# Solves and states of a tile moved into the first half of the next turn, behind the next tile's first Gram

## The chip, the core and the metric

The kernel runs on one core of one Trainium2 chip. The metric is device time of one execution in microseconds (us): the median of three runs, beside one profiled execution whose trace is read here. Engines: PE (TensorE) multiplies, PEld is its weight load, DVE (VectorE) and POOL (GpSimd) do elementwise work, ACT (ScalarE) activations and copies out of PSUM, SP issues the DMAs of this stage.

## What is computed

One inference step of a hybrid decoder layer over 1024 prompt tokens and 64 sample tokens (8 sequences of 8), all fp32, D_MODEL 1024:

```python
proj = rmsnorm(x) @ w_in
conv_out = swish(LayerNorm(causal depthwise conv of width 31 (GLU)))
# rwkv group, 8 heads of 64, per token t:
S_t = S_{t-1} diag(w_t) + (S_{t-1} (-kk_t)) (kk_t*a_t)^T + v_t k_t^T
y_t = S_t r_t                     # then per-head GroupNorm + bonus, output gate
x = x + concat(conv_out, rwkv_out) @ w_out
x = x + HierMoE(RMSNorm(x))       # 32 experts, top-2 in the top-1 group
```

The change lies wholly in the stage that computes the recurrence S_t, y_t. The recurrence is done in chunks of 64 tokens: within a chunk a unit triangular matrix is built from products of the keys (a Gram matrix) and inverted, and then the chunk's corrections u, its outputs y and the new state follow from a few 64x64 products per head.

## The kernel before

Programs of the engines are written out by hand; their order is the order of the calls, and semaphores tie them. After the input projection a loop of **turns** works on tiles of 128 tokens (NT - 1 = 8 tiles of the prompt, and tile 8 with the 64 sample tokens). In turn j (`turn(j)`, one function of that name on each engine) four tiles are in work:

- tile j + 1: `decay`, `iclr`, `key_norms`, `cumulate` on PE, `decay_tanh`, `iclr_tanh`, `norms_wide`, `exps`, `key_scale` on ACT, `decay_add`, `keys`, `scaled_a_b` on DVE, `scaled_r_k` on POOL. The last two make the operands of the next turn's Gram; PE waits for them in `scaled_ready`.
- tile j: `gram_and_values` (first Gram, banks 2 and 3, and value transposes, bank 0), `first_level` and `first_gb` on DVE, the key Gram and `key_tokens`. The 16x16 diagonal blocks of its triangular matrix are inverted on DVE (`small_blocks`, `whole_blocks`), with SP carrying them out to DRAM and back in another layout (`invert_blocks(j)`: 8 stores at L604, 2 loads at L608, then, when `blocks_turned` on ACT is done, 2 stores at L613 and 8 loads at L618).
- tile i = j - 1: with its inverted blocks in place (`inv_in`), two levels of doubling make the inverse of 64x64 (called level 4 and 5; PE products, DVE `level_masks`, ACT `x_copies`). Then a chain in two chunks: PE `first_u`, ACT `u_copy`, PE `first_state`, DVE `new_state`, PE `second_rhs`, ACT `rhs_copy`, PE `second_u`, ACT `u_copy`, PE `second_state`, ACT `y_copy`.
- tiles j - 2 and j - 3: GroupNorm (`gn_centre`, `gn_square`, `gn_variance`, `gn_root`, `gn_inverse`, `y_scaled`), `to_channels`, `gn_affine`, the bonus and the `gate`.

On PE all solves, state and output products go through L1704 (`product`), Grams are L1730, transposes into tokens L1716, decay and iclr L1568 and L1574, `key_norms` L1582, `cumulate` L1659. On DVE: `level_masks` L2636, `keys` L2473 and L2478, `small_blocks` L2650 and L2652, `new_state` L2674 and L2677, `whole_blocks` L2661 to L2669, `scaled_a_b` L2487 and L2492, `gn_centre` L2684 and L2685, `gn_variance` L2692. On ACT: `exps` L1132 to L1134, `key_scale` L1065, `u_copy` L1232, `blocks_turned` L1077, `gn_root` L1249 (a Sqrt, for which ACT loads another table), `norms_wide` L1072, `tok_copy` L1210. On POOL: `scaled_r_k` L848 to L860, `r_times_k` L885, `y_plus_bonus` L898.

Turn j of PE ends with the chain of tile j - 1, and turn j + 1 begins with `scaled_ready` and the first Gram of tile j + 1; then PE needs the inverted blocks of tile j (`level_in`, `inv_in`). ACT's `blocks_turned(j)` stands near the end of turn j, behind `exps`, `key_scale` and the second `u_copy`. DVE's `whole_blocks(j)` uses the tile MM as scratch and so waits for the last read of MM by PE.

## Time and profile before

| | us |
|---|---|
| median of 3 runs (lowest, highest) | 1180.27 (1179.73, 1181.55) |
| the profiled execution | 1184.61 |
| its span, first to last instruction | 1182.8 |
| PE busy | 1074.6 (91%) |
| DVE, ACT, POOL busy | 665.6, 356.4, 213.6 |
| mean granted TensorE clock, as a share of 2.4 GHz | 0.959 |

The turns lie between 386 and 617 us of the span; before them is the input projection, behind them the output projection and the experts. The page gives the busy share of each engine in 40 slices of 29.6 us, and the clock that PE was granted; the trace gives every instruction with its start, its length and what released it. The fall of the clock to a half is seen as a PEclk of 0.50 over a short window. Between the profiled execution and the median lie 4.3 us.

### The profile page before, as it was taken

The numbers are of one execution on the slowest core, as the hardware profiler recorded it, in microseconds if no ns is written. First come the engines' busy times: TensorE is split into PE (matmuls) and PEld (weight loads), VectorE is DVE, ScalarE is ACT, GpSimd is POOL, SyncE is SP. The second block draws the span as 40 slices with busy tenths as digits, with TensorE's granted clock in tenths as the row PEclk, the third lists the DMA queues.
The fourth block names the chain that finished last, engine by engine and source line by source line (L and its number), as shares of the span: only waits on it lengthen the run. The fifth ranks groups of instructions, "written<-read, shape, count | busy, mean of one in ns | idle before, by whom it ended". The sixth has DMA issues, their size and how long they took to land.

```text
span 1182.8 us, 24194 instructions
## 1 busy us (share of the span) xinstructions
PE 1074.6 (91%) x9392; PEld 636.7 (54%) x9393; DVE 665.6 (56%) x1136; ACT 356.4 (30%) x691; POOL 213.6 (18%) x278
## 2 busy tenths in 40 slices
PE   7999999999997767777689999985999999999986
PEld 5666666666665766766685455554333333333342
DVE  6388999973668666666543321456434343343416
ACT  6000011101335555555432221113132323222324
POOL 4000000000011312222220011001333333242110
PEclk9999999999998888898999999986999999999999
DMA  9211111100000111111124322138898889999839
GB/s 277 65 35 36 36 36 44 33 27 22 1 1 8 23 21 19 18 19 20 20 48 188 106 63 71 45 120 339 326 377 317 323 311 342 414 406 404 329 115 389
DMA packets 97790, 171.44 MB, mean 145 GB/s; under 512 B 44490, under 2 KB 69249, under 8 KB 88419
## 3 DMA queue, kind: packets, MB, share of 16 engines
q1 hardware_dynamic: 90211, 152.31, 36.2%
q0 software_dynamic: 7488, 17.84, 4.3%
q8 instruction: 66, 1.08, 0.4%
q14 instruction: 25, 0.20, 0.1%
HBM read 153.64 MB, written 25.91 MB: 152 GB/s over the span
## 4 chain that ended last, share of the span: by engine, by line
PE 79%; DMA 8%; DVE 4%; SPq 3%; ACT 3%; issue 2%; POOLq 0%; DVEq 0%; ACTq 0%
PE ps L1688 27%; PE ps L2306 13%; PE ps L2156 9%; PE ps L2336 7%; PE ps L1704 7%; SPq L618 2%; DMA arena<-y_rows 2%; PE ps L2293 2%; DMA arena<-in_w_exp_up_dram 2%; DMA x_blocks<-arena 2%; PE ps L2186 1%; DMA arena<-x_blocks 1%; PE ps L1730 1%; DMA arena<-in_w_exp_down_dram 1%; ACT arena L1065 1%
## 5 line engine op out<-in xcount | busy, mean ns | idle before, releaser
L1688 PE MATMUL ps<-arena 128*128 128x384 f32 (+1 forms) x1032 | 316.6, 468 | 0.0
L1688 PEld LDWEIGHTS ps<-arena 128*128 128x128 f32 x1032 | 195.3, 190 | 118.0 <-issue 1.9
L2306 PE MATMUL ps<-arena 128*64 x416 | 188.5, 596 | 3.0 <-DVE arena L3040 1.4
L2309 PE MATMUL ps<-arena 128*64 128x512 f32 x416 | 188.5, 596 | 0.0
L2458 DVE SCALAR_TENSOR_TENSOR arena<-arena,cw 128x1024 f32<-128x1024 f32 x240 | 168.2, 777 | 0.4
L1704 PE MATMUL ps<-arena 64*64 64x64 f32 x2960 | 101.9, 240 | 57.6 <-DMA arena<-x_blocks 35.9
L1704 PEld LDWEIGHTS ps<-arena 64*64 64x64 f32 x2960 | 92.9, 153 | 63.8 <-issue 44.1
L2306 PEld LDWEIGHTS ps<-arena 128*64 128x64 f32 x416 | 54.4, 136 | 111.8 <-issue 111.6
L2156 PE MATMUL ps<-arena 128*128 128x512 f32 x256 | 113.1, 596 | 0.0
L2336 PE MATMUL ps<-arena 128*64 x208 | 96.5, 607 | 2.4 <-ACT arena L1443 2.4
L2339 PE MATMUL ps<-arena 128*64 128x512 f32 x208 | 96.5, 607 | 0.0
L2156 PEld LDWEIGHTS ps<-arena 128*128 128x128 f32 x256 | 47.5, 190 | 57.1 <-issue 57.0
L964 POOL DMA_INDIRECT late<-xn_rows,g_idx x24 | 65.9, 2744 | 20.4 <-POOL g_idx L961 20.4
L870 POOL COPY lastz<-arena 128x1 f32<-128x1 f32 x14 | 11.4, 813 | 318.0 <-ACT arena L1161 318.0
L1155 ACT ACTIVATE arena<-ps 128x768 f32<-128x768 f32 x14 | 11.4, 812 | 178.6 <-PE ps L1688 178.6
L3061 DVE COPY arena<-arena 128x4096 f32 x26 | 59.4, 2283 | 8.5 <-SPq L707 6.7
L3046 DVE TENSOR_TENSOR small<-ps,small 128x256 f32<-128x256 f32 x26 | 11.0, 424 | 89.6 <-ACT small L1427 89.6
L2336 PEld LDWEIGHTS ps<-arena 128*64 128x64 f32 x208 | 26.8, 138 | 53.0 <-issue 53.0
L3070 DVE COPY arena<-ps 128x256 f32<-128x256 f32 x26 | 11.0, 424 | 78.1 <-PE ps L2322 78.1
L1443 ACT ACTIVATE arena<-arena 128x2048 f32 x26 | 49.6, 1908 | 17.5 <-SPq L711 16.3
L2309 PEld LDWEIGHTS ps<-arena 128*64 128x64 f32 x416 | 54.4, 136 | 0.0
L1730 PE MATMUL ps<-arena 64*64 64x128 f32 x544 | 41.6, 313 | 6.9 <-DVE arena L2492 6.9
(370 smaller groups left out, 1490.3 us busy)
## 6 DMA issues: line engine op xcount, KB each, us to landing
arena<-in_w_exp_gate_dram SPq DMA_DIRECT2D x32, 1024.0 KB
arena<-in_w_exp_up_dram SPq DMA_DIRECT2D x32, 1024.0 KB
arena<-in_w_exp_down_dram SPq DMA_DIRECT2D x32, 1024.0 KB, 9.4
arena<-in_w_in_dram SPq DMA_DIRECT2D x22, 512.0 KB, 4.1
arena<-in_x_prompt_dram SPq DMA_DIRECT2D x16, 512.0 KB, 8.2
arena<-y_rows SPq DMA_DIRECT2D x8, 1024.0 KB, 16.3
arena<-in_w_out_dram SPq DMA_DIRECT2D x2, 2048.0 KB
xn_rows<-arena SPq DMA_DIRECT2D x8, 512.0 KB, 2.9
```

Source lines behind the costliest of these rows:

```text
L964: pool.indirect_dma_start(out=xg[b], out_offset=None, in_=xn2_rows, in_offset=bass.IndirectOffsetOnAxis(ap=g_idx[b][:, :], axis=0), bounds ...
L1443: act.activation(wd.rearrange("p c n -> p (c n)"), wring[:, bass.ds(slot, 1), 2 * DC * F:].rearrange("p a n -> p (a n)"), ACT.Copy)\
L1688: ins = pe.matmul(banks(proj_bank(q) + piece)[:, 0:n1 - n0], win[q % 6][:, c, :], xnT[:, c, n0:n1], start=(c == 0), stop=(c == DC - 1))
L1704: ins = pe.matmul(dst[h, hp * 64:hp * 64 + 64], lhs[k, hp, :], rhs[k, hp, :], start=alone or (first and hp == 0), stop=alone or last, skip ...
L1730: ins = pe.matmul(banks(2 + c)[half(p), hp * P:(hp + 1) * P], lhs[h, hp, t], AR[j % 3][h, hp, :, t], start=True, stop=True)
L2156: ins = pe.matmul(banks(2 * (i % 2) + half)[0:r, :], lhs, wout[c // CT][:, c % CT, half * 512:half * 512 + 512], start=(c == 0), stop=(c = ...
L2306: pe.matmul(banks(b)[0:HS, :], xgT[b][:, c, 0:HS], wring_gu[:, bass.ds(slot, 1), 0:2, c, :].rearrange("p a w f -> p (a w) f"), start=(c == ...
L2309: ins = pe.matmul(banks(b)[HS:P, :], xgT[b][:, c, HS:P], wgu[b][:, :, c, :], start=(c == 0), stop=(c == DC - 1))
L2336: pe.matmul(banks(5 + half)[0:HS, :], hT[:, c, 0:HS], wring[:, bass.ds(slot, 1), n0:n0 + 512].rearrange("p a n -> p (a n)"), start=(c == 0 ...
L2339: ins = pe.matmul(banks(5 + half)[HS:P, :], hT[:, c, HS:P], wd[:, c, half * 512:half * 512 + 512], start=(c == 0), stop=(c == 1))
L2458: dve.scalar_tensor_tensor(out=dst, in0=src, scalar=w, in1=dst, op0=ALU.mult, op1=ALU.add).then_inc(conv_tap, 1)
L3061: dve.tensor_copy(wgu[b].rearrange("p w c f -> p (w c f)"), wring[:, bass.ds(slot, 1), 0:2 * DC * F].rearrange("p a n -> p (a n)"))\
```

## The change

- The chain of tile m = j - 2 (u, state, y of both chunks) is issued in a new first half of turn j, not in the second half of turn j - 1. PE's order there: `scaled_ready(j)`, first Gram and values of tile j, `chain_u`, `chain_state`, decay and iclr of tile j + 1, `chain_rhs`, `second_u`, `to_channels(j - 3)`, `bonus(j - 1)`, `second_state`, `gate(j - 3)`, `key_norms(j + 1)`, then level 4 of tile j - 1.
- ACT's `blocks_turned(j - 1)` moves to the first half of turn j, behind `u_copy`, `gn_root`, `norms_wide` and `tok_copy`.
- DVE: `new_state` of tile j - 2 around `first_gb(j)`; `bonus_v`, `keys` and `gated` ahead of the level 5 masks; `gn_centre` behind them; `scaled_a_b(j + 1)` between `small_blocks(j)` and `whole_blocks(j)`.
- POOL: `r_times_k` ahead of `y_scaled`.
- Tiles that now live longer get another buffer: a third value and a third GB1 tile, a fourth e_last; `whole_blocks` gets scratch of its own and no longer waits for PE; the decay product goes to bank 4, the gate to bank 0. The constant headmean, which nothing used, goes, with its three memsets.
- The last turn of the prompt has both: the chain of tile 6 in its first half and, as before, that of tile 7 in its second.

```diff
 # PE
+            def chain_u(m):
+                pe.wait_ge(rhs_done, n + 1)
+                pe.wait_ge(x_done, level_count(m, 5, 1))
+                pe.wait_ge(tok_done, 3 * m + 5)
+                for hp in range(CT):
+                    ins = solve_u(m, 0, hp)
+            def chain_state(m):
+                pe.wait_ge(u_done, n + 1)
+                for hp in range(CT):
+                    rhs_keys(m, 1, hp)
+                    ins = state_u(m, 0, hp)
+            def chain_rhs(m):
+                pe.wait_ge(gb_done, m + 3)
+                pe.wait_ge(s_done, n + 2)
+                for hp in range(CT):
+                    y_keys(m, 0, hp)
+                    ins = rhs_state(m, 1, hp)
+                ins.then_inc(rhs_psum, 1)
+                pe.wait_ge(rhs_psum, n + 2)
+                for hp in range(CT):
+                    y_state(m, 0, hp)
+                    y_keys(m, 1, hp)
+                for hp in range(CT):
+                    ins = y_u(m, 0, hp)
+            def first_half(j):
+                m = j - 2
+                scaled_ready(j)
+                if j < NT - 1:
+                    gram_and_values(j)
+                else:
+                    gram(j, bt, gb_psum)
+                if j >= 2:
+                    chain_u(m)
+                    chain_state(m)
+                if j < NT - 1:
+                    if j == 1:
+                        pe.wait_ge(cvar_done, len(PIECES))
+                    if j >= 4:
+                        pe.wait_ge(aff_done, j - 3)
+                    decay(j + 1, decay_bank(j + 1))
+                    pe.wait_ge(kk_done, 2 * j + 1)
+                    iclr(j + 1)
+                if j >= 2:
+                    chain_rhs(m)
+                    second_u(m)
+                if j < NT - 1:
+                    if j >= 3:
+                        pe.wait_ge(decay_sum, j + 2)
+                        to_channels(j - 3, 4)
+                    bonus(j - 1)
+                if j >= 2:
+                    second_state(m)
+                if 3 <= j < NT - 1:
+                    pe.wait_ge(tok_done, 3 * j + 1)
+                    gate(j - 3, 0)
             def turn(j):
-                scaled_ready(j)
-                gram_and_values(j)
-                pe.wait_ge(kk_done, 2 * j + 1)
-                pe.wait_ge(s_sum, n)
-                decay(j + 1, decay_bank(j + 1))
-                iclr(j + 1)
+                first_half(j)
+                pe.wait_ge(iclr_done, j + 2)
+                key_norms(j + 1)
+                pe.wait_ge(decay_sum, j + 2)
+                pe.wait_ge(rk_used, j)
...
                 pe.wait_ge(tok_done, 3 * j + 1)
+                if j >= 3:
+                    pe.wait_ge(mix_done, j - 2)
                 key_tokens(j)
...
-                pe.wait_ge(iclr_done, j + 2)
-                key_norms(j + 1)
                 level_x(i, 5)
-                first_u(i)
-                if j >= 3:
-                    to_channels(j - 3, 4)
-                else:
-                    bonus(i)
-                first_state(i)
-                if j >= 3:
-                    bonus(i)
-                second_rhs(i)
+                pe.wait_ge(tok_done, 3 * j + 3)
                 cumulate(j + 1)
-                second_u(i)
-                if j >= 3:
-                    gate(j - 3, 4)
-                second_state(i)
 # ACT
+            def first_half(j):
+                m = j - 2
+                if j >= 2:
+                    u_copy(2 * m)
+                if j >= 3:
+                    gn_root(j - 3)
+                if j == 3:
+                    conv_root(2)
+                if j < NT - 1:
+                    norms_wide(j + 1)
+                    tok_copy(j, 0, value_rows(j), 0)
+                if j >= 2:
+                    blocks_turned(j - 1)
+                if j < NT - 1:
+                    iclr_tanh(j + 1)
+                if j >= 2:
+                    rhs_copy(2 * m + 1)
+                if j < NT - 1:
+                    decay_tanh(j + 1)
+                if j >= 2:
+                    y_copy(m, 0, 2)
+                    u_copy(2 * m + 1)
+                    if 3 <= j < NT - 1:
+                        gn_affine(j - 3, 4)
+                    y_copy(m, 1, 3)
 # DVE
             def turn(j):
                 first_level(j, mask_ar)
+                if j >= 2:
+                    new_state(j - 2, 0)
                 first_gb(j, mask_ar)
-                level_masks(j - 1, 4)
+                if j >= 3:
+                    gn_inverse(j - 3)
                 decay_add(j + 1)
                 if j >= 2:
-                    gn_centre(j - 2)
+                    new_state(j - 2, 1)
+                bonus_v(j - 1)
+                level_masks(j - 1, 4)
+                keys(j + 1)
                 if j >= 3:
-                    gn_inverse(j - 3)
+                    gated(j - 3, 0)
                 masked_k(j, mask_ar)
                 level_masks(j - 1, 5)
-                keys(j + 1)
+                if j >= 2:
+                    gn_centre(j - 2)
                 small_blocks(j)
-                new_state(j - 1, 0)
+                scaled_a_b(j + 1)
                 whole_blocks(j)
-                bonus_v(j - 1)
-                scaled_a_b(j + 1)
-                new_state(j - 1, 1)
-                if j >= 3:
-                    gated(j - 3, 4)
                 if j >= 2:
                     gn_variance(j - 2)
```

## Rows read from the trace of the kernel before

**Rows 1.** The page, second part: PE's granted clock in 40 slices, in tenths.
```profile
PEclk9999999999998888898999999986999999999999
```

**Rows 2.** Waits from 410 to 592 us: who for whom, us, times, longest.
```profile
PE ps L1704 <- DMA arena<-x_blocks: 35.7, 7, 6.5
```

**Rows 3.** Windows: stretch, its us, busy (x) of PE, PEld, DVE, ACT, POOL, PEclk.
```profile
418.60:446.00 27.40, 19.30 (x618) 17.87 (x622) 17.98 (x41) 15.68 (x35) 4.42 (x4) 0.87 0.13 20
446.00:591.30 145.30, 106.32 (x3236) 98.33 (x3236) 95.34 (x215) 80.95 (x184) 39.60 (x36) 0.91 0.12 19
591.30:616.60 25.30, 24.66 (x632) 23.32 (x632) 9.46 (x19) 10.45 (x27) 7.42 (x6) 0.89 0.26 51
```

**Rows 4.** Timeline of turn 5: PE's first level-4 product, SP's issues; landing of L608.
```profile
504.47 1.34 PE L1704 MATMUL ps<-arena 64*64 64x64 f32 x35 [4.77 <-DMA arena<-x_blocks]
...
499.07 3.75 SPq L618 DMA_DIRECT2D arena<-x_blocks  x8
...
509.01 1.15 SPq L608 DMA_DIRECT2D arena<-u_blocks  x2
...
528.77 2.27 SPq L618 DMA_DIRECT2D arena<-x_blocks  x5
...
DMA to landing us min/median/max: 2.0/2.7/3.8
```

**Rows 5.** Timeline of DVE in turn 5: start, us, line, tiles, idle before and releaser.
```profile
508.15 0.69 DVE L2685 SCALAR_TENSOR_TENSOR arena<-arena 128x512 f32<-128x512 f32 x1
...
510.95 0.89 DVE L2636 TENSOR_TENSOR arena<-ps,mask_lv 128x256 f32<-128x256 f32 x2 [0.25 <-PE ps L1704]
...
513.83 0.17 DVE L2650 TENSOR_TENSOR arena<-arena 128x12 f32<-128x12 f32 x1
...
516.18 0.17 DVE L2652 TENSOR_TENSOR arena<-arena 128x12 f32<-128x12 f32 x1
...
517.83 1.64 DVE L2663 TENSOR_TENSOR arena<-arena 128x256 f32<-128x256 f32 x1
...
519.96 0.59 DVE L2663 TENSOR_TENSOR arena<-arena 128x256 f32<-128x256 f32 x1
...
521.01 0.41 DVE L2669 TENSOR_REDUCE arena<-arena 64x32 f32<-64x256 f32 x1
...
524.42 0.68 DVE L2492 SCALAR_TENSOR_TENSOR arena<-arena 128x512 f32<-128x512 f32 x1
...
528.60 0.67 DVE L2692 TENSOR_REDUCE arena<-arena 128x8 f32<-128x512 f32 x1
```

**Rows 6.** Timeline of ACT around the end of turn 5.
```profile
522.00 0.60 ACT L1132 ACTIVATE arena<-ps 128x512 f32<-128x512 f32 x1 [0.43 <-PE ps L1659]
...
523.45 1.64 ACT L1065 ACTIVATE arena<-arena,om_ka,prm 128x128 f32<-128x128 f32 x4
524.99 0.38 ACT L1232 ACTIVATE arena<-ps 128x256 f32<-128x256 f32 x1
525.25 0.63 ACT L1077 ACTIVATE arena<-arena 64x256 f32<-64x256 f32 x1
...
527.02 1.28 ACT L1249 ACT_TABLE_LOAD   x1
529.31 0.30 ACT L1249 ACTIVATE arena<-arena,stat 128x8 f32<-128x8 f32 x1 [1.01 <-DVE arena L2692]
...
530.03 0.58 ACT L1210 ACTIVATE arena<-ps 128x512 f32<-128x512 f32 x1
```

**Rows 7.** Timeline of POOL in turn 5.
```profile
517.76 1.27 POOL L898 TENSOR_TENSOR arena<-arena 128x512 f32<-128x512 f32 x1 [6.43 <-ACT arena L1258]
...
525.17 1.27 POOL L853 TENSOR_TENSOR arena<-arena 128x512 f32<-128x512 f32 x1 [0.63 <-ACT arena L1065]
```

**Rows 8.** Windows over first Gram and values, in turns 1 and 2, at either clock.
```profile
386.20:389.80 3.60, 3.60 (x65) 3.27 (x65) 0.97 (x2) 1.81 (x3) 3.15 (x3) 0.50 0.21 21
410.80:412.70 1.90, 1.90 (x74) 1.73 (x68) 1.66 (x2) 0.90 (x2) 1.82 (x3) 1.00 0.26 71
```

## What was expected of the change

> **What bounds the kernel now.** I read the page's slices first. PE is busy nearly everywhere, but in the stage of the turns its granted clock is below full in most slices [rows 1], and only there does the clock fall again and again. Next the waits of that stage: PE waits 35.7 us in 7 pieces for the inverted blocks that SP brings back from DRAM [rows 2]. Then the windows: from one level 4 to the next, turn 2 takes 27.4 us and turns 3 to 7 take 145.3 us, 29.06 each, of which PE is busy 106.32 us, 73%, at a mean clock of 0.91; turn 8 has no such wait left in it, 24.66 of 25.3 us are busy [rows 3]. So in turns 2 to 7 PE's work is not the limit, a loop is, and the reader finds it by following the blocks. In turn 5 (I write T for the start of level 4, 504.47): the loads of the inverse began 5.40 us earlier; the second trip of SP, which brings the raw blocks, starts at T + 4.54 [rows 4]; DVE's level 5 masks end at T + 7.4, after them come the keys, `small_blocks` starts at T + 9.36 and ends at T + 11.9, and `whole_blocks` ends at T + 16.95 [rows 5]. ACT turns the blocks only at T + 20.78 to T + 21.4, because exps, key_scale and a u_copy stand ahead of it [rows 6]; the loads start at T + 24.3 [rows 4], and 5.4 us later the next level 4 can start, T + 29.7. That is the turn. PE's idle time hides in this loop, and so does part of its half clock.
>
> **What the change does to the loop, step by step.** The same sum for a turn 3 to 6 after the change, T again at level 4.
>
> (a) Start of `small_blocks`. The raw blocks: T + 4.54, the second issue some 0.6 later, landing 2.7 after it [rows 4]: T + 7.8. DVE: the level 5 masks; keys, 1.8, and the gate product, 0.6, are moved ahead of them, but into time in which DVE waited for PE, and PE has lost nothing there except that `key_tokens` now waits for `gated`. I lay these at T + 4.2 for the gate product, 5.3 for the tokens, 6.9 for the end of the masks (estimate: 7.4 in rows 5 with the first 3.4 us at half clock, less 1.2 for that, plus 0.7 for the new wait). Then `gn_centre`, 1.3 (two operations like the one in rows 5). T + 8.2, so DVE and not the DMA decides, by 0.4. Bounds 7.8 and 9.4 (as before).
>
> (b) `small_blocks`, 2.4 (513.83 to 516.35) [rows 5]: T + 10.6.
>
> (c) `scaled_a_b`, new at this place, 2 operations of 0.68 overlapping a little [rows 5], 1.3: T + 11.9. It needs the exps, and these need `cumulate`, which PE can now issue right behind level 5, about T + 7.4 to 8.5; exps until T + 10.1. They are ready. PE's next turn starts here, because `scaled_ready` waits for it: PE is idle from T + 8.5 to T + 12.
>
> (d) `whole_blocks`. In turn 5 it takes 3.8 us (517.62 to 521.42) though one of its two equal multiplications took 1.64 and the other 0.59 [rows 5]: the long one began at 517.83 and ended 0.44 behind POOL's operation, which ran from 517.76 to 519.03 [rows 7]. Bare, it is 2.8. Moved, it lies at T + 11.9, and key_scale ends at T + 11.6 (exps at 10.1 and 1.64 [rows 6]); 0.08 behind that start POOL's two products of `scaled_r_k`, 1.27 each [rows 7], then `r_times_k`. So where there was one overlap there are now two or three: 0 to 2.1 us, and I take 2.1, since the start of the POOL operation follows key_scale by a fixed 0.08 and the copy and first multiplication fall just behind it. T + 16.8. The Trainium skill (SBUF — State Buffer, section Practical consequences) says why, and speaks against this place: a DVE instruction with two SBUF inputs contends with a GpSimd instruction that reads SBUF, and the later one is blocked to the end of the first. By that rule the 2.1 is due in full; had the rule no hold here the sum would be 2.1 less. The trace agrees with it, 1.64 against 0.59.
>
> (e) `gn_variance` 0.65 [rows 5], and ACT's `gn_root` with `norms_wide`, `tok_copy` and `blocks_turned` behind it: from 529.27 (end of the variance) to 530.61 [rows 5, 6] and another 0.63, 2.0. T + 19.5.
>
> (f) SP: stores, loads, landing: 2.9 (525.88 to 528.77) and 5.4 [rows 4, 6], 8.3. T + 27.8.
>
> There is a second path into (e), through PE and ACT, and it is the one that I trust least. `blocks_turned` stands behind `u_copy(2m)`, and that behind the first Gram: T + 12, Gram and values 1.9 at full clock or 3.6 at half [rows 8], the solve 0.6 to 1.1, the copy 0.5 with its latencies [rows 6], the table load of 1.28 that follows [rows 6], then the 2.0 of (e): T + 18.3 or T + 20.4; with (f) T + 26.6 or T + 28.7. Will the clock be half there? PE's idle time of 3.5 us is shorter than the 4.77 us that came before a fall [rows 4], and longer than any ahead of the Gram of turn 2, which ran at full clock [rows 8]. I expect a fall in part of it, and a turn of **28.2 us**, between 27.8 and 28.7.
>
> PE's own path has more air: `chain_rhs` starts when DVE is through with the variance, `first_level`, `new_state` and `first_gb`, about T + 19.8; then the rhs copy (behind `iclr_tanh` in ACT's queue, T + 23.2), the second solve, the u copy at T + 25, `new_state` and `bonus_v` until T + 27.1, gate and key_norms until T + 27.6. 0.6 us ahead of the blocks. The idle 4.8 us of PE are thus filled with the chain, but two other waits (3.5 and 1.2 us, with 0.5 before `first_gb`) take their place. The waits that are added for bank 4 and bank 0 (`aff_done`, `decay_sum`) end earlier than this and cost nothing; the memsets taken out stand in the start and cost or give nothing.
>
> **The sum over the turns.** Turn 2: no gate product and one more small root, 27.9 against 27.4. Turns 3 to 6: 28.2. Turn 7: the next tile has 64 tokens, so scaled_a_b and POOL's products are half as long, and norms_wide and tok_copy are not ahead of `blocks_turned`: 25.6. Together 27.9 + 4 * 28.2 + 25.6 = 166.3, against 27.4 + 145.3 = 172.7: -6.4. Turn 1 loses nothing of its chain (tile 0's goes to turn 2), its key norms and bonus come ahead of level 4, +1.8, but `blocks_turned(1)` has no root ahead of it: I get level 4 of turn 2 1.4 us earlier. Turn 8 is PE work, 24.66 of 25.3 us at a mean clock of 0.89 [rows 3]; its level 4 began behind 6.5 us of idle time [rows 2], now about 3: of the loss of 2.8 (0.11 * 25.3) I count half as regained, -1.4. Sum -9.2. What follows (output projection, routing, experts) waits for nothing with a date of its own, its loads hang on this stage's semaphores, so all of it is passed on: 1184.6 - 9.2 = 1175.4 for the execution as profiled, and from the median 1180.3 - 9.2 = **1171**. The first is 4.3 above the second before the change; I keep that distance.
>
> **The rivals.**
> - *The overlaps do not come and the clock holds.* Then (d) costs 2.8 and the PE path decides, T + 26.6: 5 * 26.6 + 24.4 = 157.4, -15.3, with -1.4 and -2.8, -19.5: 1161. For it: in rows 7 POOL's start hangs on ACT, and 0.3 us of shift would let DVE go first. Against: the idle 3.5 us of PE.
> - *The loop stays as long as it was.* Half clock in all of the chain and small_blocks only at T + 8.9: the turn stays near 29, the six sum to 172, and turn 8 gives nothing: with turn 1 some 1178, 1177 to 1180. For it: before the change, too, the loop went through DVE, ACT and SP, none of which gets less work. That the gain is made but not passed on to the end would look the same.
> - *Slower: the first Gram ahead of the solve.* PE could solve tile m at T + 8.5, where all inputs are there, but must wait for `scaled_a_b`, and ACT's table load and `blocks_turned` queue behind the copy of that solve. If small_blocks starts at T + 9.4 as before, PE starts at T + 13.1, and with half clock: 3.6, 1.1, 0.5, 1.3, 2.0 and 8.3 make T + 29.9. Five of these and one of 27.5 make 177, +4.3, and turn 1 gives nothing either: 1185. It decides as soon as the first solve's copy ends after T + 18 or so, against T + 17.2 in my sum.
>
> **How the numbers follow.** The forecast, own range 1167 to 1176, 0.45; the fast case 0.20; the unchanged one 0.17; the slower one 0.15; 0.03 for cases between the first two. A measurement of this kernel can tell about 0.2%, 2.4 us, from no change, so faster begins at 1177.9: of the unchanged case 0.03 lies below that and 0.01 above 1182.7. Faster 0.71, same 0.13, slower 0.16. Leaving out one in ten at either end, the range is 1160 to 1183.
>
> **What would show it.** Right: level 4 starts 28.2 us apart; PE's longest idle time in a turn lies before the first Gram and is about 3.5 us, released by DVE L2492; its wait for x_blocks is near 1 us; the copy and multiplications of `whole_blocks` are stretched beside POOL's products; turn 8 starts at full clock. Wrong: small_blocks later than T + 8.5, for then (a) is mis-sized; blocks turned later than 2.0 us behind `gn_variance`, for then ACT's queue holds them; or turns of 30 us with the wait for x_blocks still 4 us.

## The result, and the profile after

| | before | after |
|---|---|---|
| median of the runs beside each other | 1180.91 (1179.73 to 1182.38, 4 runs) | 1200.62 (1199.03 to 1203.87, 4 runs) |
| the profiled execution, its span | 1184.61, 1182.8 | 1201.09, 1199.3 |
| mean granted clock | 0.959 | 0.952 |
| the end of turn 8 in the span | 616.5 | 633.6 |

The changed kernel is slower: 1.017 times the time before, interval 1.0145 to 1.0195, some 20 us. The spans differ by 16.5 us, and at the end of turn 8 the difference is already 17.1, so all of it arises in the turns, and what follows passes it on but for 0.6 us. The traces are of single executions: that of the kernel before lies 4.3 us over its median and that of the kernel after 0.5, so the medians differ by 19.7 us where the traces differ by 16.5. The page of the kernel after:

```profile
PE 1083.2 (90%) x9392; PEld 643.5 (54%) x9393; DVE 676.3 (56%) x1136; ACT 356.8 (30%) x691; POOL 214.9 (18%) x275
...
PEclk9999999999997988888899999995999999999999
```

The clock row answers rows 1: it still falls in the slices of the turns. DVE's work is busy for 676.3 us where it was 665.6, though it computes the same; the extra time will turn up below. Next PE's waits from 405 to 640 us (for whom, us, times, longest), beside rows 2:

```profile
PE ps L1746 <- DVE arena L2554: 31.4, 7, 6.8
PE ps L1720 <- DMA arena<-x_blocks: 7.3, 6, 2.9
PE ps L1720 <- ACT arena L1232: 7.1, 5, 1.7
PE ps L1720 <- DVE arena L2684: 5.0, 6, 2.4
```

The wait for the inverted blocks, 35.7 us before, is down to 7.3. In its place the first Gram (L1746) waits 31.4 us in 7 pieces for `scaled_a_b` (L2554), and the chain behind it waits for the rhs copy (L1232) and `first_gb` (L2684). A new wait is as large as the old one, and the others come on top. The windows beside rows 3, turn 2, turns 3 to 7 and turn 8 (stretch, us, busy and count of PE, PEld, DVE, ACT, POOL, granted clock), and two short ones that are used below:

```profile
422.40:454.00 31.60, 23.10 (x654) 21.47 (x654) 21.34 (x42) 17.12 (x39) 8.02 (x7) 0.85 0.11 17
454.00:610.80 156.80, 110.12 (x3184) 100.74 (x3184) 100.96 (x214) 78.47 (x178) 38.90 (x34) 0.86 0.11 18
610.80:633.60 22.80, 22.20 (x632) 20.93 (x632) 9.35 (x17) 10.46 (x27) 6.38 (x5) 1.00 0.26 50
564.50:568.50 4.00, 3.93 (x74) 3.93 (x76) 3.79 (x8) 0.00 (x0) 1.14 (x1) 0.50 0.02 4
510.60:514.00 3.40, 3.40 (x68) 3.28 (x64) 0.00 (x0) 2.36 (x7) 0.00 (x0) 0.50 0.27 25
```

Turns 2 to 7 take 188.4 us for 172.7 before, 31.4 each for 28.8: +15.7. Of it 7.6 is PE's busy time, for nearly the same number of products (3838 for 3854) at a lower clock (133.2 busy for 125.6; 0.85 and 0.86 for 0.87 and 0.91), and 8.1 is more idle time. Turn 8 takes 22.8 for 25.3, now at full clock: -2.5. Level 4 of turn 2 comes 3.9 later than before (422.45 for 418.58). Together 17.1, which is the whole difference.

**One turn.** The turn in which level 4 starts at T = 549.02. DVE's timeline, with the columns of rows 5:

```profile
561.15 1.70 DVE L2549 SCALAR_TENSOR_TENSOR arena<-arena 128x512 f32<-128x512 f32 x1
562.77 1.75 DVE L2554 SCALAR_TENSOR_TENSOR arena<-arena 128x512 f32<-128x512 f32 x1
564.55 1.13 DVE L2721 COPY arena<-arena 64x32 f32<-64x32 f32 x1
565.72 0.59 DVE L2723 TENSOR_TENSOR arena<-arena 128x256 f32<-128x256 f32 x1
...
567.85 0.41 DVE L2729 TENSOR_REDUCE arena<-arena 64x32 f32<-64x256 f32 x1
568.29 0.69 DVE L2752 TENSOR_REDUCE arena<-arena 128x8 f32<-128x512 f32 x1
```

and POOL's (beside rows 7) over the same time:

```profile
561.04 1.26 POOL L857 TENSOR_TENSOR arena<-arena 128x512 f32<-128x512 f32 x1 [1.10 <-ACT arena L1068]
562.38 1.59 POOL L864 TENSOR_TENSOR arena<-arena 128x512 f32<-128x512 f32 x1
563.93 1.71 POOL L889 TENSOR_TENSOR arena<-arena 128x512 f32<-128x512 f32 x1
```

The two operations of `scaled_a_b` take 1.70 and 1.75 where rows 5 has 0.68, and the copy of `whole_blocks` behind them 1.13 (0.18 in the next turn shown). DVE and POOL are slow together: L2549 ends at 562.85, POOL's L864 runs from 562.38 to 563.97, L2554 ends at 564.52, POOL's L889 begins at 563.93. Both are longer than where the other engine is silent. In the turn with T = 484.41 the same three products of POOL start later, at 499.66, and hit the multiplications of `whole_blocks` (L2723) instead, 1.56 and 1.09 for 0.59 bare:

```profile
498.89 0.68 DVE L2554 SCALAR_TENSOR_TENSOR arena<-arena 128x512 f32<-128x512 f32 x1
499.60 0.18 DVE L2721 COPY arena<-arena 64x32 f32<-64x32 f32 x1
499.82 1.56 DVE L2723 TENSOR_TENSOR arena<-arena 128x256 f32<-128x256 f32 x1
501.41 0.42 DVE L2727 TENSOR_REDUCE arena<-arena 128x32 f32<-128x256 f32 x1
501.86 1.09 DVE L2723 TENSOR_TENSOR arena<-arena 128x256 f32<-128x256 f32 x1
```

PE and ACT in the turn of T = 549.02 (the two engines' timelines, beside rows 6):

```profile
564.57 0.48 PE L1746 MATMUL ps<-arena 64*64 64x128 f32 x2 [6.75 <-DVE arena L2554]
```

```profile
568.99 0.38 ACT L1237 ACTIVATE arena<-ps 128x256 f32<-128x256 f32 x1 [7.51 <-PE ps L1720]
569.39 1.28 ACT L1254 ACT_TABLE_LOAD   x1
570.68 0.30 ACT L1254 ACTIVATE arena<-arena,stat 128x8 f32<-128x8 f32 x1
...
571.89 0.64 ACT L1080 ACTIVATE arena<-arena 64x256 f32<-64x256 f32 x1
```

PE idles 6.75 us ahead of the first Gram, then runs at half clock (the window from 564.5 to 568.5 shows 0.50). So it is in every one of the turns 2 to 7: most or all of the 4 us from the first Gram on are at 0.50, where before the change that Gram was at full clock in each of them. The Gram, the values and the solve end 4.4 us later, `u_copy` (L1237) can only then start, the table load of 1.28 is queued behind it though ACT had been idle for 7.51 us, and `blocks_turned` (L1080) ends at 572.53, 4.3 behind the end of `whole_blocks` (568.26). SP's issues, beside rows 4:

```profile
572.56 1.28 SPq L618 DMA_DIRECT2D x_blocks<-arena  x2
575.42 4.42 SPq L623 DMA_DIRECT2D arena<-x_blocks  x8
```

The eight loads take 4.42 to issue, 3.75 before. The turn is 32.5 long.

**All turns.** To compare kernels I took the same stations from every timeline, counted from DVE's first level-4 mask (some 0.8 to 1.2 behind PE's level 4), and averaged turns 2 to 6 of the one profiled execution of each kernel (among the runs below that execution lies between 5 us under the kernel's median and the median itself); us:

| | small_blocks starts | takes | scaled_a_b takes | whole_blocks takes | whole ends | then turned | then loads start | loads take | then next mask | turn |
|---|---|---|---|---|---|---|---|---|---|---|
| before | 8.8 | 2.5 | (1.6) | 3.6 | 15.9 | 3.2 | 3.1 | 3.75 | 2.9 | 28.9 |
| as predicted | 7.4 | 2.4 | 1.3 | 4.9 | 16.0 | 2.7 to 3.6 | 2.9 | 3.75 | 2.45 | 28.2 |
| after | 7.8 | 3.1 | 2.3 | 4.3 | 18.0 | 3.8 | 2.9 | 4.35 | 2.7 | 31.7 |
| e4_pool_small | 8.1 | 2.55 | 1.3 | 2.8 | 14.9 | 5.2 | 2.9 | 4.6 | 2.5 | 30.0 |
| e11_pool_wait_only | 7.75 | 3.55 | 1.3 | 2.8 | 15.4 | 4.9 | 2.9 | 4.4 | 2.7 | 30.35 |
| e3_no_idle | 8.0 | 3.95 | 1.9 | 4.1 | 18.1 | 3.1 | 2.9 | 4.5 | 2.8 | 31.35 |
| e2_turned_first | 7.8 | 3.5 | 1.9 | 4.5 | 17.8 | 0.8 | 2.9 | 4.9 | 4.1 | 30.5 |
| e1_solve_first | 7.8 | 3.3 | 2.0 | 4.5 | 17.9 | 2.6 | 2.9 | 4.55 | 2.7 | 30.6 |
| e12_turned_wait | 7.6 | 3.35 | 1.4 | 2.8 | 15.4 | 2.4 | 2.9 | 4.5 | 4.5 | 29.6 |
| e14_clock_wait | 7.8 | 3.3 | 1.4 | 2.8 | 15.5 | 3.4 | 2.9 | 4.7 | 2.7 | 29.2 |
| e9_pool_waits | 7.6 | 3.3 | 1.4 | 2.8 | 15.2 | 0.7 | 2.9 | 4.4 | 4.9 | 28.1 |

A mean of "then next mask" above 3 means that in most of the turns PE was not ready when the blocks were. Of the changed kernel's five turns it is one, with 4.2; in the other four it is 2.3 to 2.5, and the blocks came last. Before the change `scaled_a_b` had another place, hence the brackets.

### The profile page after: what moved, and what is told of

The parts are those of the page before. It is cut to its first block, busy times and chain, and to the rows that moved or that the text cites. A ratio compares the mean times of both kernels' runs of the same rounds, so it can differ in the third digit from the quotient of the medians.

```text
span 1199.3 us, 24204 instructions
## 1 busy us (share of the span) xinstructions
PE 1083.2 (90%) x9392; PEld 643.5 (54%) x9393; DVE 676.3 (56%) x1136; ACT 356.8 (30%) x691; POOL 214.9 (18%) x275
## 3 DMA queue, kind: packets, MB, share of 16 engines
q1 hardware_dynamic: 90211, 152.31, 35.7%
## 4 chain that ended last, share of the span: by engine, by line
PE 77%; DMA 7%; DVE 6%; SPq 3%; issue 3%; ACT 2%; POOL 0%; POOLq 0%; DVEq 0%; ACTq 0%
PE ps L1704 26%; PE ps L2368 14%; PE ps L2218 9%; PE ps L2398 8%; PE ps L1720 3%; PE ps L1746 2%; SPq L623 2%; PE ps L2355 2%; DMA arena<-y_rows 2%; PE ps L2248 1%; DMA arena<-in_w_exp_down_dram 1%; PE ps L1732 1%; DMA x_blocks<-arena 1%; PE ps L2384 1%; PE ps L1546 1%
## 5 line engine op out<-in xcount | busy, mean ns | idle before, releaser
L2368 PEld LDWEIGHTS ps<-arena 128*64 128x64 f32 x416 | 54.5, 136 | 112.2 <-issue 112.1
L1720 PE MATMUL ps<-arena 64*64 64x64 f32 x2960 | 94.7, 232 | 21.1 <-DMA arena<-x_blocks 7.3
L1720 PEld LDWEIGHTS ps<-arena 64*64 64x64 f32 x2960 | 86.4, 145 | 27.8 <-issue 10.6
L1746 PE MATMUL ps<-arena 64*64 64x128 f32 x544 | 48.3, 343 | 39.5 <-DVE arena L2554 38.3
L1746 PEld LDWEIGHTS ps<-arena 64*64 64x64 f32 x544 | 41.2, 175 | 42.1 <-DVE arena L2554 39.9
L2398 PEld LDWEIGHTS ps<-arena 128*64 128x64 f32 x208 | 26.8, 139 | 53.1 <-issue 53.1
```

Of the source, the lines that this page charges most:

```text
L1720: ins = pe.matmul(dst[h, hp * 64:hp * 64 + 64], lhs[k, hp, :], rhs[k, hp, :], start=alone or (first and hp == 0), stop=alone or last, skip ...
L1746: ins = pe.matmul(banks(2 + c)[half(p), hp * P:(hp + 1) * P], lhs[h, hp, t], AR[j % 3][h, hp, :, t], start=True, stop=True)
L2368: pe.matmul(banks(b)[0:HS, :], xgT[b][:, c, 0:HS], wring_gu[:, bass.ds(slot, 1), 0:2, c, :].rearrange("p a w f -> p (a w) f"), start=(c == ...
L2398: pe.matmul(banks(5 + half)[0:HS, :], hT[:, c, 0:HS], wring[:, bass.ds(slot, 1), n0:n0 + 512].rearrange("p a n -> p (a n)"), start=(c == 0 ...
```

## The experiments

The theory behind them: three things lengthen the turn, and each can be taken out. (1) POOL's products lie on the DVE work that is now in the loop. (2) `blocks_turned` hangs, through ACT's queue, on the first Gram and the solve of the same turn. (3) PE idles ahead of the first Gram, loses its clock, and that makes (2) later. The rival to each: the loop goes through something else, and the removal gives nothing. The kernel before gave 1181.1, 1181.3 and 1182.1 beside them; ratios are to it. The intervals are 2 to 5 us to either side, so a difference of two changed kernels is uncertain by 4 to 6 us.

**e1_solve_first.** The solve of tile m ahead of the first Gram, so that `u_copy` doesn't wait for `scaled_a_b`.

```diff
                 m = j - 2
+                if j >= 2:
+                    chain_u(m)
                 scaled_ready(j)
...
                 if j >= 2:
-                    chain_u(m)
                     chain_state(m)
```

> The changed kernel (1200.6 us) with one edit: chain_u (the first solve of tile m) stands ahead of the first Gram in PE's order. My theory is that the turn is set by the loop through DVE, ACT and SP, with three terms larger than in my sum: POOL's operations block small_blocks and scaled_a_b too, the clock is at half behind PE's idle time ahead of the Gram, so that the solve's copy and ACT's blocks_turned behind it are late, and SP's eight loads take longer. Then this edit takes the half-clock Gram and the solve out of ACT's path, which falls back on the end of gn_variance: some 1 us in each of six turns, 1194 us. Rival: the order Gram before solve is itself the cause, and its undoing brings back all of the 20 us, to 1181. Second rival: PE's own path to level 4 is the limit; then it brings the solve and its copy, 1.6 us per turn, 1191.

Measured: 1194.15, ratio 1.0114 (1.0076 to 1.0153), 6.5 us less than the changed kernel and as the theory had it; both rivals, 1181 and 1191, are further off. `blocks_turned` comes 1.2 us sooner behind `whole_blocks` (2.6 for 3.8), the turn is 1.1 shorter. Undone alone, the order that gives the change its name brings this much; (2) holds, but it is not the bulk.

**e2_turned_first.** ACT's order instead: `blocks_turned` right behind `u_copy`, ahead of the root and its table load.

```diff
                     u_copy(2 * m)
+                    blocks_turned(j - 1)
...
-                if j >= 2:
-                    blocks_turned(j - 1)
```

> The changed kernel with one edit: ACT's blocks_turned stands right behind the first u_copy of the turn, ahead of gn_root with its table load, norms_wide and tok_copy. SP's stores should start about 2.5 us earlier. If the inverted blocks are what the next level 4 waits for, it gains until PE's own chain is the limit, 1 to 1.3 us per turn (PE waited 9.9 us for x_blocks in seven turns): 1193 us. Rival (PE's chain is the limit, and the blocks arrive just beside it): no change, 1200, and PE's wait for x_blocks is gone.

Measured: 1189.64, ratio 1.007 (1.0048 to 1.0093), 11 us less where 7 to 8 were expected. Blocks are turned 0.8 behind `whole_blocks` for 3.8, three us sooner, but the turn is only 1.2 shorter, since now PE is late by 1.4 ("then next mask" 4.1), SP's loads take 0.5 longer and DVE's part is as long as before. PE's wait for the blocks is gone, as the rival had it, but the gain came all the same. PE's largest wait stays:

```profile
PE ps L1745 <- DVE arena L2553: 29.6, 7, 5.3
```

**e3_no_idle.** Against (3) alone: 64 filling products a turn behind `cumulate`, into a bank that nobody reads, so that PE is not idle ahead of the Gram.

```diff
                 cumulate(j + 1)
+                pe.wait_ge(x_done, level_count(i, 5, 1))
+                for _ in range(8):
+                    heads(banks(4)[:, 0:256], PT[i % 2][:, 0, :, :], XF[:, 0, :, :], alone=True)
```

> The changed kernel with 64 more 64x64 products per turn on PE behind cumulate, into bank 4, whose result nobody reads: PE is busy for some 3 us of the 3.2 to 6.8 us in which it waited for scaled_a_b. Theory: PE then keeps 2.4 GHz, first Gram, values and solve take 2.6 us and not 4.8, u_copy and with it blocks_turned come 2 us earlier: 1188 to 1190 us, granted clock of the stage near 1.0. Rival: the half clock is hidden behind DVE's whole_blocks, as my sum had it for PE's own path: 1199 to 1201 with the clock up all the same.

Measured: 1194.86, ratio 1.0099 (1.0062 to 1.0137), 5.8 us less and not the 11 expected. The clock did hold (mean 0.968 for 0.952, the first Gram at full clock in five of the turns 2 to 7), and the blocks are turned 0.7 sooner. But PE's waits behind the Gram grew:

```profile
PE ps L1720 <- DVE arena L2687: 15.0, 7, 4.1
PE ps L1746 <- DVE arena L2557: 7.9, 4, 4.4
```

A quick PE arrives at `chain_rhs` and waits there for `first_gb`, which DVE does only behind `whole_blocks` and the variance: 15.0 us for 5.0. So a part of the half clock seems to have been hidden behind DVE, and DVE's lateness had to be tested next. That (3) lengthens (2) is seen turn by turn: in the four of the five turns whose Gram ran at full clock the blocks are turned 2.6 to 2.75 behind `whole_blocks`, in the one whose Gram ran at 0.50 it is 4.9.

**e4_pool_small** and **b1_pool_small.** Against (1): POOL's four products of `scaled_r_k` and `r_times_k` work on 16 tokens of 128, in the changed kernel and in the one before.

```diff
+                w = 16 if 2 <= j < NT - 1 else r
+                tw = slice(j * P, j * P + w)
-                pool.tensor_tensor(AR[j % 3][:, :, 1, 0:r], zs[:, R0:R0 + CT, t], e_in[:, :, 0:r], ALU.mult)\
+                pool.tensor_tensor(AR[j % 3][:, :, 1, 0:w], zs[:, R0:R0 + CT, tw], e_in[:, :, 0:w], ALU.mult)\
```

(and the same for the other three)

> The changed kernel in which, for tiles 2 to 7, POOL's four products per tile (AR's second half, k times th, kt, r times k) are done on 16 of the 128 tokens only; the rest of them is left out. Each takes some 0.25 us and not 1.27. Theory: small_blocks goes back from 3.5 to 2.5 us, scaled_a_b from 1.9 to 3.4 back to 1.3, whole_blocks from 4.2 to 4.7 back to 2.8; the Gram starts 2 to 3 us earlier and all behind it: 1184 to 1188 us. Rival (the clock and the order decide, contention is beside the path): above 1195.

> The kernel before with the same reduction as e4_pool_small (POOL's four products per tile on 16 of the 128 tokens for tiles 2 to 7; the rest left out). Before, these products ran while DVE was between whole_blocks and the next masks, or idle. Theory (the overlap is new with the change): at most 0.5 us per turn, 1178 to 1181. Rival (the products cost as much before, and e4 shows no more than shorter work): some 10 us, 1171.

Measured: 1190.14, ratio 1.006 (1.0034 to 1.0087), for the changed kernel, 10.5 us less; 1181.39, ratio 1.0004 (0.9989 to 1.0019), for the kernel before, nothing. For the changed kernel this lies between the two theories (1184 to 1188, above 1195). Before the change these products, too, met DVE: `scaled_a_b` took 1.6 on the mean for 1.3. In turn 5:

```profile
523.18 1.31 DVE L2487 SCALAR_TENSOR_TENSOR arena<-arena 128x512 f32<-128x512 f32 x1 [1.04 <-issue]
```

```profile
522.68 1.27 POOL L848 TENSOR_TENSOR arena<-arena 128x512 f32<-128x512 f32 x1 [3.65 <-ACT arena L1132]
```

b1 brings it to 1.3 in every turn and the time stays, so there this overlap cost nothing; it is the change that put it on the path. The stretched `whole_blocks` of the kernel before (3.6 for 2.8) is another matter. The product beside it is `y_plus_bonus` (rows 7), which b1 leaves whole, and in b1 the multiplication is as long as it was:

```profile
517.74 1.64 DVE L2667 TENSOR_TENSOR arena<-arena 128x256 f32<-128x256 f32 x1
```

```profile
517.66 1.27 POOL L902 TENSOR_TENSOR arena<-arena 128x512 f32<-128x512 f32 x1 [7.66 <-ACT arena L1262]
```

What that one cost before wasn't tested. In e4's row of the table all three DVE stations drop to their bare length and `whole_blocks` ends 3.1 sooner, but `blocks_turned` follows it 5.2 later instead of 3.8: 1.4 of the 3.1 us are lost again, by the theory to (2) and (3).

**e7_state_turned.** Both cures of (2): solve and first state ahead of the Gram, and `blocks_turned` early as in e2.

```diff
                     u_copy(2 * m)
+                    blocks_turned(j - 1)
...
+                if j >= 2:
+                    chain_u(m)
+                    chain_state(m)
                 scaled_ready(j)
...
-                if j >= 2:
-                    chain_u(m)
-                    chain_state(m)
```

> Two edits together on the changed kernel: PE's chain_u and chain_state ahead of the first Gram (one step more than e1_solve_first), and ACT's blocks_turned right behind the first u_copy (e2_turned_first). With the blocks early (e2) PE waits no longer for them, so its own path from scaled_a_b to level 4 is the turn; taking solve, copy and state out of it is 0.6 + 0.5 + 0.75 us at full clock and up to 3 at half, six times: 1189.6 - 11 to -18, 1172 to 1179 us. Rival (chain_rhs waits for first_gb, which DVE reaches only behind whole_blocks, so that the PE path loses nothing): 1186 to 1189.

Measured: 1191.37, ratio 1.0096 (1.0059 to 1.0133); no better than e2, and 2 us above what even the rival gave. The rival held. PE's waits (same view as above):

```profile
PE ps L1719 <- ACT arena L1237: 22.7, 8, 3.4
PE ps L1719 <- DVE arena L2683: 15.5, 7, 4.8
```

The wait for `scaled_a_b` is gone, and two others stand in its place: 22.7 us for `u_copy`, and 15.5 us for `first_gb` (L2683), the end of DVE's queue. The first isn't free: in four of the seven turns `scaled_a_b` was ready 0.9 to 1.6 us before the Gram began. But PE waits for `first_gb` behind it in any case. Once ACT is out of the way, DVE, stretched by POOL, is the limit through PE's chain; e9 tests that.

**e9_pool_waits** and **e11_pool_wait_only.** POOL's two key products are held back until `whole_blocks` is done, in e7's order (e9) and in the order of the change (e11). Nothing is left out and nothing shortened.

```diff
                 pool.wait_ge(kk_done, 2 * j + 2)
+                if 2 <= j:
+                    pool.wait_ge(blk_done, 2 * j - 1)
                 link(pool.tensor_tensor(zs[:, K0:K0 + CT, t], zs[:, K0:K0 + CT, t], th[:, :, 0:r], ALU.mult))
```

> e7_state_turned and one wait more: POOL's second and third operation of scaled_r_k (k times th, kt) wait until whole_blocks is done. No work is left out. whole_blocks should fall from 4.2 to 4.7 us to 2.8, and DVE reach first_gb 1.5 us earlier. If first_gb is what chain_rhs waits for: 6 to 9 us less than e7, some 1168. Rival (the first Gram's start sets PE's path, not first_gb): equal to e7 within 2 us.

> The changed kernel with that wait of POOL alone. It takes the overlap out of whole_blocks but leaves those in small_blocks and scaled_a_b, and it leaves the half clock. blocks_turned hangs on the Gram and the solve there, so theory says little: chain_rhs 1.5 us earlier in turns where it waited for first_gb, 1197 to 1200 us. Rival (whole_blocks is on the path as in my forecast's sum (d)): 2 us per turn, 1188.

Measured: e9 **1175.05** (1173.16 to 1178.48, 6 runs), ratio 0.996 (0.9938 to 0.9981): faster than both kernels. e11 1190.56, ratio 1.0104 (1.0062 to 1.0147). The wait takes 16.3 us from e7, twice what was expected, and 10.1 from the changed kernel, where 1 to 4 were expected: the rival, `whole_blocks` on the path (1188), is nearer. That is as much as e4 gave by shortening the work, so it is the overlap that costs and not POOL's work. DVE in a turn of e11:

```profile
491.65 1.13 DVE L2716 TENSOR_TENSOR arena<-arena 128x24 f32<-128x24 f32 x1
...
493.66 0.69 DVE L2551 SCALAR_TENSOR_TENSOR arena<-arena 128x512 f32<-128x512 f32 x1
494.27 0.68 DVE L2556 SCALAR_TENSOR_TENSOR arena<-arena 128x512 f32<-128x512 f32 x1
494.99 0.18 DVE L2723 COPY arena<-arena 64x32 f32<-64x32 f32 x1
495.20 0.58 DVE L2725 TENSOR_TENSOR arena<-arena 128x256 f32<-128x256 f32 x1
```

and POOL:

```profile
491.47 1.28 POOL L852 TENSOR_TENSOR arena<-arena 128x512 f32<-128x512 f32 x1 [13.32 <-ACT arena L1137]
...
497.88 1.27 POOL L859 TENSOR_TENSOR arena<-arena 128x512 f32<-128x512 f32 x1 [4.99 <-DVE arena L2731]
```

Every operation beside which POOL is silent has its bare length, 0.69, 0.68, 0.18, 0.58. The one small operation of `small_blocks` that meets POOL's L852, which the wait doesn't hold back, takes 1.13 for 0.18. e9's waits and windows (the turns from level 4 of turn 2, and turn 8):

```profile
PE ps L1721 <- ACT arena L1239: 22.6, 8, 3.4
PE ps L1721 <- DVE arena L2685: 12.2, 7, 4.5
```

```profile
418.40:584.40 166.00, 126.59 (x3830) 115.52 (x3830) 112.88 (x257) 95.18 (x217) 43.71 (x41) 0.90 0.12 20
584.40:607.00 22.60, 22.07 (x656) 20.91 (x647) 9.09 (x17) 10.99 (x29) 6.38 (x5) 1.00 0.29 57
```

Six turns take 166.0, the 166.3 of my sum, and turn 8 is at full clock. That the two sums agree is luck: the terms differ. `whole_blocks` ends at 15.2 for 16.0, the blocks are turned 0.7 behind it for some 3.1, and then PE is late, 4.9 for 2.45. (The span is 11.6 us shorter than that of before in the profiled executions, the medians differ by 6.3; the profiled one of before lay 4.3 over its median.)

**e12_turned_wait** (the wait and e2's order of ACT, Gram still first) and **e14_clock_wait** (the wait and e3's filling products) split the rest. Each is two of the edits above together.

> The changed kernel with two edits: POOL's wait for whole_blocks (e11_pool_wait_only, 1190.6) and blocks_turned right behind the first u_copy (e2_turned_first, 1189.6). PE's order is the changed one, first Gram ahead of the first solve. If the two cures are of the same loop through the blocks, they add: 1190.6 - 11, 1180 us, and the rest to e9_pool_waits (1175.1) is the order of Gram and solve, 5 us. Rival (PE's own path, with the first Gram ahead, already sets the turn in both): 1186 or more, and the order is worth 11 or more.

> The changed kernel with POOL's wait and with the 64 filling products per turn on PE (e3_no_idle). Alone they gave 10 and 6 us. If the clock is a cost of its own on the path Gram, solve, u_copy, blocks_turned, with e11 the Gram is no later and the path is set by it alone, so the whole 6 or more come: 1182 to 1185. Rival (e3's 6 us came from elsewhere, or the filling delays what it should speed up): 1189 or more.

Measured: e12 1183.77, ratio 1.002 (0.9998 to 1.0041), between what the two theories gave; e14 1182.48, ratio 1.0001 (0.998 to 1.0021), as the theory gave it. e12 and e9 differ by PE's order alone, and that is worth 8.7 us here; e12's blocks are turned 2.4 behind `whole_blocks`, since `u_copy` still waits for the Gram, and PE still waits for `scaled_a_b`:

```profile
PE ps L1747 <- DVE arena L2555: 25.4, 7, 4.2
```

e14 against e11: the filling products are worth 8.1 us where POOL's wait has taken the overlap off `whole_blocks`, and 5.8 (e3) where it has not; the runs do not tell the two apart. The window over e14's turns shows the clock, 0.96 for the 0.86 of the change:

```profile
423.00:600.00 177.00, 146.65 (x4660) 136.09 (x4661) 114.15 (x255) 97.44 (x223) 44.08 (x41) 0.96 0.15 26
```

**e10_all_clock.** e9 with 32 filling products, to see whether the clock still costs anything there.

> e9_pool_waits (1175.1: solve and state ahead of the Gram, blocks_turned early, POOL's wait) with 32 filling products per turn on PE behind cumulate. What PE still waits for there is a copy (22.6 us in eight pieces) and first_gb (12.2). If half clock still costs in it: 1170 to 1173. Rival (in e9 the Gram stands behind a wait that hides the half clock, and the filling now delays the solve ahead of it by 1 us per turn): 1176 to 1182.

Measured: 1177.88, ratio 0.9982 (0.9962 to 1.0001), 2.8 above e9, where the intervals still touch, and in the rival's range. The filling gives nothing here. The likely reason, not tested by itself, is that with the solve first it stands in front of work that sets the turn.

**What adds up.** From 1200.6: the wait of POOL -10.1, `blocks_turned` early -11.0, the clock -5.8, the solve ahead of the Gram -6.5; each alone. Two at a time: wait and early -16.9 for 21.1, wait and clock -18.1 for 15.8; neither differs from its sum by more than the runs' noise. PE's order on top of early (with the first state, too, ahead of the Gram) gives nothing without the wait (e7 against e2: 1.7 slower, within the spread of the runs) and 8.7 with it; wait, early and order together -25.6. So no single part of the change is the cause: each repair gives only a part, and behind it another path ends last (PE in e2, ACT in e4 and e11).

## Why the prediction was wrong

I forecast 1171 and 9.2 us of gain; the change costs 20 us, outside the range. Between the traces it is -9.2 forecast and +16.5 measured. Of these 25.7 us turns 2 to 7 make 22.1 (+15.7 for -6.4), turn 1 5.3, turn 8 -1.1 and the rest of the kernel -0.6. The steps that failed are (b) and (c), the overlap with POOL that I laid on `whole_blocks` alone, and (e), where I let the Gram run at half clock in part of the turns only, and so took the path through it and ACT's queue for the shorter one in the rest.

**What bounds the turn** was right: a loop through DVE, ACT and SP, its length passed on to the end (17.1 of difference behind turn 8, 16.5 in the span). **Turn 8** was the right mechanism and a little short: full clock, 22.8 for 25.3, -2.5 where I had -1.4.

**(a)** was 0.4 short: `small_blocks` starts at 7.8 in the table's count for 7.4, or some T + 8.6, just past the T + 8.5 that I gave as a sign of being wrong.

**(b), (c)** mis-sized. I laid POOL's products only on `whole_blocks`, from a path in which key_scale ends 0.3 us ahead of it. They fall on all three: `small_blocks` 3.1 for 2.4 (the first product, which hangs on the exps alone), `scaled_a_b` 2.3 for 1.3, up to 3.4 in the turn shown. The 2.4 was a slip besides: 513.83 to 516.35 is 2.5. And the trace of before had the overlap of (c) in it, L2487 with 1.31 for 0.68 beside L848 (shown with b1); I took the bare length. **(d)** itself was foreseen, and somewhat over: 4.3 for 4.9. With (a) and 0.35 of gaps between them `whole_blocks` ends at 18.0 for 16.0, the largest part of the 3.5 us by which the turn missed. The Trainium skill (SBUF — State Buffer, section Who interferes with whom, under "Practical consequences"), on which I weighed (d), says that a DVE instruction with two SBUF inputs contends with a GpSimd instruction that reads SBUF. The operations of `scaled_a_b` are such instructions too, and the trace agrees with 1.70 and 1.75 for 0.68: I had the rule and applied it to one place. The same list says that `tensor_reduce` never contends on this chip and that a `copy` can; the trace agrees, with L2727 at its bare 0.42 at 501.41 beside POOL's L864, and the copy at 1.13 for 0.18.

**(e)** I named two paths and set the forecast between them, with half clock "in part of it". The half clock came in every turn, and in full. I had taken an idle time of 3.5 us for too short to bring it surely. PE idled 4.5 us on the mean (31.4 in 7), since (b) and (c) made `scaled_a_b` late, but the clock did not need that to fall: in two of the turns 2 to 7 it idled only 3.19 us, and the Gram behind ran at 0.50 all the same. So the second path, through `u_copy` and the table load, ended last in every turn. Blocks turned 3.8 behind `whole_blocks`, for some 3.1 in my sum (halfway from 2.7 to 3.6): +0.7. The half-clock case by itself, 3.6, was nearly right. The sign of being wrong that I gave for this came, too: in the turn of T = 549.02 the blocks are turned 3.55 behind the end of `gn_variance`, for 2.0.

**(f)** 2.9 was right; the eight loads took 4.35 for 3.75: +0.6, in the mean of every kernel with the new order, and not explained. The last 0.3 of the 3.5 lie between the loads and the next mask, 2.7 for 2.45, and come from the one turn in which PE was late.

**PE's own path**, for which I left 0.6 us of air, was used up. In the turn with T = 484.41 the blocks were there and PE was not: level 4 of the next turn starts without a wait at 517.66, 33.25 us on, behind a second fall of the clock (0.50 from 510.6 to 514.0) after a wait for the rhs copy. That wait has ACT's queue in it, where `iclr_tanh` with a second table load stands ahead of the copy:

```profile
507.65 1.28 ACT L1092 ACT_TABLE_LOAD   x1
508.94 1.14 ACT L1092 ACTIVATE arena<-ps,prm 128x128 f32<-128x128 f32 x4
509.96 0.40 ACT L1232 ACTIVATE arena<-ps 128x256 f32<-128x256 f32 x1
```

```profile
510.41 0.27 PE L1720 MATMUL ps<-arena,gain 64*64 64x64 f32 x2 [1.66 <-ACT arena L1232]
```

I had this order in my sum, but not that such waits (7.1, 5.0) could cost the clock again. It is one turn of the five averaged; the rhs copy ahead of `iclr_tanh` wasn't tried.

**Turn 1**: level 4 of turn 2 came 3.9 late; I had it 1.4 early. The repairs give it back in part or in whole: DVE's first mask of turn 2 lies at 419.8 before, 423.6 after, 422.0 in e3, 421.7 in e11, 420.8 in e1 and e2, 420.5 in e4, 419.5 in e9 and e12. So turn 1 suffers from the same as the others; the 1.4 of gain comes in none.

**The rival** "the first Gram ahead of the solve" named the right mechanism, with 1185 and a chance of 0.15. It was priced as one late path with everything else as in the sum, 29.9 a turn; e1 gives 6.5 us for its cure alone. What made it 31.4, as I read the runs, is that the overlap with POOL and the clock feed that path: lateness of `scaled_a_b` is idle time of PE, half clock follows the idle time, and half clock is lateness of `u_copy`. I had the terms of all three and gave each its own case, as if they excluded each other.

The sign, then, hung on three orders: POOL's products, bound to exps and key_scale, the root ahead of `blocks_turned` in ACT's queue, and the Gram ahead of the solve. With all three turned, the half turn's shift brings 0.4% (e9). Whether the rest is in PE's waits for `first_gb` (12.2 us in e9) wasn't tried.

## What to carry to other kernels

When work is moved into the loop that sets the time, list for its new place every instruction of POOL that can run at the same time, and price the overlap for each DVE instruction with two SBUF inputs, not for one of them: the same products of POOL cost nothing in their old place (b1) and 10 us in the new one (e4, e11). A wait of PE can cost more than its length: behind the 3.2 to 6.8 us ahead of the first Gram PE ran 4.0 us at 0.50. So put work whose inputs are long there (the old tile's solve) ahead of work that is still waited for (the new tile's Gram). And where several paths are within a microsecond of each other, test repairs together: alone each gave 6 to 11 us, POOL's wait, the blocks early and the solve first together 25.6, and of all that was tried only these three together made the kernel clearly faster than before.

## What the runs showed of the hardware

- A chain of DVE operations beside back-to-back operations of POOL (1.27 us bare) paid 1.0 to 1.1 us for each of its own in the turn shown: 1.70 and 1.75 for 0.68. POOL is stretched too, 1.59 and 1.71 for 1.27. A small operation on 24 columns pays as much as a large one, 1.13 for 0.18 (e11).
- PE's granted clock stood at 0.50 for the whole 4.0 us behind 3.19, 4.48, 5.3 and 6.75 us of idle time ahead of the first Gram. In e3, where the filling products left at most 1.5 us of such idle time in five of the turns 2 to 7, the Gram ran at full clock in these; in the sixth PE still idled 4.4 us, and the Gram ran mostly at half.
- Filling products that nobody reads can pay: 64 a turn gave 5.8 (e3) and 8.1 us (e14 against e11). In e9's order 32 of them gave nothing (2.8 us more, within the spread).
- In the new order SP takes longer to issue the same eight loads, 4.35 for 3.75. In the changed kernel 6 of the 64 issues took 1.1 to 1.5 us where the others take 0.45; in the kernel before the longest took 0.98 and the next 0.52. Its cause stays open; no run was made on it.
